# Order edits in a hybrid mLSTM / Mamba-2 layer: turns of one head, state copies, score weights, group sums, half-spreading products and the last row sums

## What is computed

```python
u = modulate(rmsnorm(x)); x = x + 0.5 * g1 * swiglu(u)          # ff1, 1024 x 2816
u = modulate(rmsnorm(x))
q, k, v, mo, i, f, z, xbc, dt, ga, gb = split(u @ w_in)
q, k = silu(conv4(q, k));  h = mlstm(q, k, v, i, f, state)       # 4 heads, 256 x 512 memory
h = (h - mean) * rsqrt(var + eps) * head_g * sigmoid(mo);  ya = h @ w_pa
x_, B, C = silu(conv4(xbc)); y = ssd(x_, dt, A, B, C, state) + D * x_   # 4 groups of 8 heads
y = y * silu(z); y = y * rsqrt(mean(y*y per group of 512) + eps) * norm_g; yb = y @ w_pb
x = x + g2 * ((sigmoid(ga) * ya + sigmoid(gb) * yb) @ w_out)
u = modulate(rmsnorm(x)); x = x + 0.5 * g3 * swiglu(u)           # ff2
y_out = rmsnorm(x, final_norm)                                   # plus the new states
```

## Time and profile before

| | |
|---|---|
| median of 3 runs | 1263.19 us (1263.02 to 1265.1) |
| the profiled execution's own time | 1262.8 us |
| its span in the profile | 1261.1 us |
| TensorE matmul busy | 1240.4 us, 98% of the span |
| VectorE, ScalarE, POOL busy | 62%, 49%, 18% |
| granted TensorE clock, mean | 0.993 of full speed |

### The profile page before, as it was taken

The page is one execution under the profiler, slowest core; times in us unless marked ns, Lnnn a source line. Parts: engine busy times, 40 slices in busy tenths (PEclk is TensorE's granted clock), DMA queues, the critical chain, the costliest instruction groups (busy, mean ns, idle before and its releaser), DMA issues. The chain is left out here.

```text
span 1261.1 us, 22606 instructions
## 1 busy us (share of the span) xinstructions
PE 1240.4 (98%) x9059; PEld 1144.7 (91%) x9059; DVE 783.3 (62%) x1345; ACT 620.8 (49%) x1102; POOL 220.8 (18%) x385
## 2 busy tenths in 40 slices
PE   8999999999999999999999999999999999999997
PEld 5999989998988777779999989989999999999997
DVE  4744444547976667675388787875676885455432
ACT  5523324335668555655356776565543453333432
POOL 5100000012640212130033333414200300000000
PEclk8999999999999999999999999999999999999998
DMA  9998879553324788986474558365454454653541
GB/s 310 264 345 261 260 252 300 158 167 127 117 85 145 254 299 306 355 272 173 140 206 129 158 153 243 105 206 155 127 138 152 152 190 145 200 160 111 161 138 42
DMA packets 258629, 241.54 MB, mean 192 GB/s; under 512 B 8205, under 2 KB 242141, under 8 KB 258526
## 3 DMA queue, kind: packets, MB, share of 16 engines
q1 hardware_dynamic: 249850, 211.16, 54.6%
q0 software_dynamic: 8576, 28.91, 6.8%
q10 hardware_dynamic: 100, 0.04, 0.0%
HBM read 209.88 MB, written 30.21 MB: 190 GB/s over the span
## 5 line engine op out<-in xcount | busy, mean ns | idle before, releaser
L2552 DVE TENSOR_TENSOR w_lo<-ring,w_hi 128x1024 fp32r<-128x1024 f32 (+1 forms) x264 | 337.6, 1279 | 354.4 <-ACT w_hi L1889 353.8
L1889 ACT ACTIVATE w_hi<-ring 128x1024 fp32r<-128x1024 f32 (+1 forms) x264 | 289.6, 1097 | 485.7 <-PE bank L1010 441.7
L1010 PE MATMUL bank<-u_hi,w_hi 128*128 128x320 f32 x1472 | 257.5, 316 | 0.7 <-ACT w_hi L1889 0.5
L1010 PE MATMUL bank<-u_hi,w_lo 128*128 128x320 f32 x1472 | 247.0, 310 | 0.4 <-DVE w_lo L2552 0.4
L1010 PE MATMUL bank<-u_lo,w_hi 128*128 128x320 f32 x1472 | 246.4, 310 | 0.0
L1010 PEld LDWEIGHTS bank<-u_hi,w_hi 128*128 128x128 f32 x1472 | 222.8, 188 | 16.3 <-issue 9.6
L1010 PEld LDWEIGHTS bank<-u_hi,w_lo 128*128 128x128 f32 x1472 | 223.7, 188 | 1.3 <-DVE w_lo L2552 1.2
L1010 PEld LDWEIGHTS bank<-u_lo,w_hi 128*128 128x128 f32 x1472 | 224.3, 188 | 0.1
L818 POOL TENSOR_TENSOR arena<-x_t,gain 128x64 f32<-128x64 f32 x16 | 4.8, 298 | 337.4 <-DVE x_t L2634 337.4
L1010 PE MATMUL bank<-ff_hi,w_hi 128*128 128x320 f32 x352 | 57.5, 310 | 0.0
L1010 PE MATMUL bank<-ff_hi,w_lo 128*128 128x320 f32 x352 | 56.8, 308 | 0.0
(11 more groups left out here) (426 smaller groups left out, 1682.1 us busy)
## 6 DMA issues: line engine op xcount, KB each, us to landing
ring<-in_w_in SPq DMA_DIRECT2D x52, 1024.0 KB, 5.4
ring<-in_ff_w SPq DMA_DIRECT2D x44, 1024.0 KB, 7.5
ring<-in_ff_w SPq DMA_DIRECT2D x32, 704.0 KB, 4.7
arena<-in_ada_w SPq DMA_DIRECT2D x20, 1024.0 KB, 10.0
ring<-in_ada_w SPq DMA_DIRECT2D x16, 1024.0 KB, 11.9
arena<-in_state_mlstm_C SPq DMA_DIRECT2D x22, 512.0 KB, 6.6
out_s_C<-arena POOLq DMA_DIRECT2D x22, 512.0 KB, 6.9
ring<-in_w_pa SPq DMA_DIRECT2D x8, 1024.0 KB, 8.0
```

Of the source, the lines that this page charges most:

```text
L1010: return nc.tensor.matmul(dst, lhs, rhs, start=first, stop=last)
L1889: nc.scalar.activation(w_hi[v.split_no % 2][:, 0:v.kc, :], panel_part(v), ACT.Copy).then_inc(S["hi_done"], 1)
L2552: V.tensor_tensor(w_lo[r][:, 0:v.kc, :], panel_part(v), w_hi[r][:, 0:v.kc, :].bitcast(FP32), ALU.subtract)\
```

## The change

It moves work, adds no instruction and takes none away. `i` is the place of a unit in its stage.

1. Stage 3 of the heads: head 2's tiles 8 to 11 are turned, gated and split at `i` = 4, 5, 6, 7, where it was 3, 4, 5, 6.
2. TensorE, groups: `head_outputs` stands ahead of `pack_inputs` (i = 2) and of `grown_decays` (i = 3).
3. VectorE, groups, i = 1: `sample_masks` stands behind `weights` and `outputs`.
4. ScalarE, i = 4, units other than `xbc` (only stage 3): `old_states(gr, 0)` stands ahead of the gate copy.
5. Tail: `group_sums(2)` moves from behind unit 3 into unit 4, behind its first eight products. `roots(0, 3)` on ScalarE and `group_roots(0, 3)` on VectorE move from unit 3's list to unit 4's. TensorE's `group_roots` stay behind unit 4.
6. End: the three products of the partly summed squares run before the wait for the last square, the other three after it; tile 1 comes last.

```diff
-TURN_SLOTS = ({}, {3: 0, 4: 1, 5: 2}, {0: 3, 3: 4, 4: 5, 5: 6}, {0: 7, 3: 8, 4: 9, 5: 10, 6: 11})
+TURN_SLOTS = ({}, {3: 0, 4: 1, 5: 2}, {0: 3, 3: 4, 4: 5, 5: 6}, {0: 7, 4: 8, 5: 9, 6: 10, 7: 11})
...
                     if i == 1 and gr > 0:
                         turn_old_part(gr - 1)
+                    if 1 <= i <= 4:
+                        head_outputs(gr, i - 1)
                     if i == 2:
                         pack_inputs(gr)
                     if i == 3:
                         grown_decays(gr)
-                    if 1 <= i <= 4:
-                        head_outputs(gr, i - 1)
...
             for i, u in enumerate(tail_units()):
-                dense(u)
+                dense(u, inner=(lambda: group_sums(2)) if i == 4 else None)
...
                 if i == 3:
                     group_sums(1)
-                    group_sums(2)
...
-            pe.wait_ge(S["sq_ready"], 4 * KD)
-            for c in range(3):
-                rows = 128 if c < 2 else 64
-                t = slice(c * 128, c * 128 + rows)
-                mm(aux[3][0:rows, c:c + 1], sq[:, 0, t], ones[:, 0:1], True, False)
-                ins = mm(aux[3][0:rows, c:c + 1], sq[:, KD - 1, t], ones[:, 0:1], False, True)
+            for kc in (0, KD - 1):
+                if kc > 0:
+                    pe.wait_ge(S["sq_ready"], 4 * KD)
+                for c in (0, 2, 1):
+                    rows = 128 if c < 2 else 64
+                    t = slice(c * 128, c * 128 + rows)
+                    ins = mm(aux[3][0:rows, c:c + 1], sq[:, kc, t], ones[:, 0:1], kc == 0 and c == 0, kc > 0 and c == 1)
...
                     high_ahead(u)
+                    if i == 4 and u.name != "xbc":
+                        old_states(gr, 0)
...
-                    if i == 4:
+                    if i == 4 and u.name == "xbc":
                         old_states(gr, 0)
...
-                if i == 3:
+                if i == 4:
                     roots(0, 3)
-                if i == 4:
                     squares(3)
...
-                    if i == 1:
-                        if gr > 0:
-                            old_part(gr - 1)
-                        sample_masks(gr)
+                    if i == 1 and gr > 0:
+                        old_part(gr - 1)
                     if i < 4 and not amid:
                         weights(gr, i)
                     if 1 <= i <= 3 and not amid:
                         outputs(gr, i - 1)
+                    if i == 1:
+                        sample_masks(gr)
...
-                if i == 3:
+                if i == 4:
                     group_roots(0, 3)
```

## The result

The changed kernel takes 1271.4 us (median of 4 runs, 1270.81 to 1272.56); the kernel before, on the same chip, 1263.51 us (4 runs, 1263.02 to 1265.1). The ratio is 1.0061, 95% interval 1.0044 to 1.0079: slower by 0.61%, 7.7 us (the medians differ by 7.9). The profiled execution of after took 1270.81 us with a span of 1268.8 us, 7.7 above the span before.

A forecast was written before the change was run, and what follows sets the result against it. TensorE, its matmul row busy 98% of the span, was taken as the bound, so time changes only where it stands still or runs slowly. Terms summed to +5.1 on the profiled 1262.8: 1267.9 us, range 1264.0 to 1270.2.

The forecast's parts named there:

- turns of head 2: Heads: new waits of 1.55 before the second `pa` unit and 1.8 before head 3's turns, 0.85 gained; net +2.55 us.
- clock behind it: Head 3's turns: the clock falls to half after the new waiting; +1.65 us, bounds 0 and 3.3.
- head outputs, masks: Groups, i = 2: the wait goes on both sides, 0.3 to 0.5 in each of four groups; -1.6 us.
- state copies: Group 3: the copy ahead of the gate removes the 1.01 us wait of `turn_states(3, 1)`; -1.1 us.
- tail, what goes: Tail: the idle 0.73 before the third group of sums and unit 4's half clock go; -2.4 us.
- tail, the wait: Tail, behind unit 4: TensorE waits for roots and reciprocals that stand behind unit 4's rounding and gate; +5.0 us.
- tail, clock behind it: Tail: the clock falls again behind the 5 us wait; +1.65 us, bounds 0.5 and 3.3.
- end: End: half of the 12 row-sum instructions move into the idle 1.30 ahead of the last square; -0.65 us.
- the rival that it is kept: Head 3's turns: the waits come but the clock stays full, dense work between them; 1266.3 us, chance 0.28.
- The rival that the `pick_x` products wait: Groups: masks end later than 737.1, so the half-spreading products wait in their new place; 1269.5 us, chance 0.09.
- roots in time: Tail: roots are ready before unit 4 ends, TensorE goes straight on; 1261.3 us, chance 0.09.
- A drain beside the table load: Tail wait: each of two table switches costs a drain beside its load; +2.8, 1270.7 us, chance 0.04.

The follow-up runs named there:

- Experiment 2: The changed kernel with the roots and reciprocals of groups 0 to 2 ahead of the rounding in unit 4's lists of the tail: 1261.96 us, ratio 0.9985.
- experiment 3: Also "wait filled": the changed kernel with 32 dense products, results unread, between unit 4 and the root products of the tail: 1268.19 us, ratio 1.0035.
- experiment 4: Also "unit 5 first": the changed kernel, with TensorE running unit 5 behind the same tail wait and the root products after it: 1270.06 us, ratio 1.0048.
- A: The changed kernel with all the edits, against the kernel before: 1271.4 us, ratio 1.0061.
- experiment 5: Also "roots before gate": the changed kernel with the tail's roots between unit 4's rounding and its gate copy, reciprocals likewise: 1270.28 us, ratio 1.0049.
- experiment 6: The kernel before with only head 2's turns moved to units 4 to 7: 1265.97 us, ratio 1.0021.
- experiment 1: Also "turns back": the changed kernel with head 2's tiles 8 to 11 back behind units 3 to 6: 1268.43 us, ratio 1.0037.
- the last kernel: The changed kernel with head 2's old turns, roots ahead of the rounding, and `grown_decays` ahead of `head_outputs` again at i = 3: 1258.51 us, ratio 0.9959.
- experiment 8: The kernel before with VectorE's order alone changed, `sample_masks` behind `weights` and `outputs`: 1266.44 us, single run.
- B: The kernel before the change: 1263.51 us, median of 4 runs beside the changed kernel.
- experiment 7: The kernel before with TensorE's order alone changed, `head_outputs` ahead of `pack_inputs` and `grown_decays`: 1266.15 us, single run.

## Why the prediction was wrong by 3.5 us, and where it was right

The forecast was 1267.9, in the range 1264.0 to 1270.2; the median is 1271.4, outside by 1.2. Slower was given 0.81 and came. The terms make 2.6 of the miss of 3.5; the rest is 0.3 of the execution's own time outside the span and 0.6 between that execution and the median. Term by term, from the shifts of the same row between the two traces:

| term | forecast | measured |
|---|---|---|
| turns of head 2 | +2.55 | +2.6 |
| clock behind it | +1.65 | 0 |
| head outputs, masks | -1.6 | -0.6 |
| state copies | -1.1 | -1.05 |
| tail, what goes | -2.4 | -2.35 (0.8 wait, 1.5 clock) |
| tail, the wait | +5.0 | +5.1 |
| tail, clock behind it | +1.65 | +4.6 |
| end | -0.65 | -0.6 |
| sum | +5.1 | +7.7 |

- **The failed step is the clock behind the tail's wait**: "the clock falls again ... so I take the seen loss, +1.65, bounds 0.5 and 3.3". The fall was right, its size was not: 4.6 lies beyond even the far bound of 3.3. I took the loss of one unit from the place where the clock fell before, though there a dense unit followed at once. Here 18 identity products follow. The clock fell at 896.9 and was back at 907.2; the work in between took 11.09 up to 908.11 in place of 6.52: 4.57 lost. Experiment 2 takes wait and clock away, 3 the clock alone; in 4, in the one execution traced, it is shorter with a dense unit first. That the wait and the clock behind it are this loss is shown; that the identity products are why the clock stays low so long rests on that one trace.
- **Clock at head 3's turns**: the rival that it is kept had 0.28 and was right; PEclk is 1.00 at both waits in A and in experiments 2 to 6, six traces. The waits are 1.66 and 1.34 with a dense unit between them. Had I taken both clock terms right, the forecast would have been 5.1 - 1.65 + 2.95 = +6.4, 1269.2. So the two errors on the clock offset each other in part: with this rival alone right, the forecast was 1266.3, further off than 1267.9.
- **Turns**: the chain of seven steps hit to 0.2 us: second `pa` unit forecast at 572.5, measured 572.68; head 3's turns 577.8 and 577.79. That the moved turns make the two waits, experiments 1 and 6 show from both sides; that it is tile 11 among the four is read from the rows (the turn at 567.02, the copy at 567.61, the gating at 571.51, the gate copy at 572.15) and was not tried alone.
- **Head outputs**: at i = 2 the wait went on both sides, 0.38 per group within the forecast 0.3 to 0.5, in three of four groups and 0.33 in the first. "At i = 3 nothing waited, so the exchange is worth 0" was wrong: 0.20 per group is lost there, which the last kernel gets back. Nothing idles in the trace at that point. In group 1 the decay rows are followed after 0.50 (743.73 to 744.23) where it was 0.41 (741.55 to 741.96), and the two `pick_b` products after 0.37 (745.15 to 745.51) where it was 0.27 (741.96 to 742.23); all other steps agree to 0.01. These two make the 0.20; why the order matters to them stays open. The rival that the `pick_x` products wait was wrong with both edits in, and is what VectorE's half alone does (experiment 8: 0.57 idle ahead of them).
- **State copies, tail what goes, end**: as forecast, to 0.05, from shifts of rows; none was tried alone. In "tail, what goes" that is partly luck. The prediction took it as given that the old wait of 0.73 costs the clock. The tail with that wait is in four traces: in B's and experiment 8's trace unit 4 then runs at half clock, in those of experiments 6 and 7 it does not (rows under "Short waits"). Against such an execution the term is worth 0.8, and only against one like B's trace 2.35.
- **The wait of the tail**: forecast T + 5.0, measured T + 5.10, with T = 891.92. The rival "roots in time" (0.09) was wrong as to this kernel; its condition, that the roots do not stand behind the rounding, is the right one: with the roots ahead of the rounding (experiment 2) the wait is gone.
- **A drain beside the table load** was wrong. The gate copy starts at 894.55 behind a load from 893.25 of 1.28, and the root at 896.30 behind one from 895.00: 0.02 left over. No drain shows, neither behind the loads nor ahead of the second, which starts 0.01 behind the end of the gate copy. The Trainium skill ("ScalarE: Activation LUTs", What ACT_TABLE_LOAD costs) puts 1.38 of drain beside the load. By an estimate from that figure, two drains would have made this wait 7.9; it is 5.1.

## What to carry to other kernels

Before an instruction is moved one place down in a list, ask whether what now stands ahead of it is a prefetch that waits for the end of the very work it should run beside; on an in-order engine a few instructions of 0.2 us then cost the full chain, here 5.1 us. Price the clock behind a wait apart from the wait, and by what runs first afterwards: here the wait of 5.1 us in front of identity products cost 4.6 more, dense work in the wait, even useless, took that away, and a dense unit directly behind it took some 2.8 of it away in the one execution traced. A half clock seen once in a trace is one execution's: see whether it comes back in others before a change is credited with removing it. Where two engines' orders are changed together, neither half can be judged alone: here each lost about 0.46 per group and both together gained 0.38.

## What the runs showed of the hardware

**How long the clock stays low.** From windows of half a microsecond, one traced execution of each kernel, with the loss taken against the 6.52 us that root products and unit 5 take at full clock (893.23 to 899.75 in experiment 2):

| kernel | idle | clock at half | runs first | half until, behind the first dense product | lost |
|---|---|---|---|---|---|
| A | 4.94 | 896.9 to 907.2 | identity | 4.8 | 4.57 |
| turns back | 4.94 | 894.1 to 904.3 | identity | 3.3 | 3.88 |
| roots before gate | 3.20 | 897.0 to 907.2 | identity | 4.1 | 4.26 |
| unit 5 first | 4.94 | 894.7 to 901.5 | dense | 4.0 | 1.79 |
| wait filled | 0.26 | never | - | - | 0.1 |

In all four the clock came back 3.3 to 4.8 us after the first dense unit began; in three of them it had stood at half through 5.3 us of identity products before that. The loss is 0.45 of the time worked at half clock in each of them (10.2, 8.6, 9.4 and 4.0 us). Where in the wait the clock falls varies too: 0.1 ahead of its end in the first row, 1.6 in the second, 0.8 in the third and 2.9 in the fourth, so the stretches of the third column also hold waiting. Why the clock did not rise during the identity products is open; it was not tried.

**Short waits.** 1.66 and 1.34 with a dense unit between them cost no clock in six traces. 0.73 between one-column products was followed by half clock in two traces (B and experiment 8) and not in two others (experiments 6 and 7). Timeline and window of TensorE in experiment 6, around the wait and unit 4:

```profile
889.58 0.81 PE L1010 MATMUL aux<-ones,arena 128*128 128x1 f32 x6 [0.73 <-POOL arena L986]
890.32 1.44 PE L1010 MATMUL bank<-u_hi,w_hi 128*128 128x320 f32 x8
```

```profile
889.00:893.00 4.00, 3.42 (x24) 1.00 0.21 62
```

So the wait is not enough by itself, and what else decides is open. In the eight traces that have a tail without that wait, no half clock stands at unit 4 before the new wait.

**The start of the kernel.** Identical code before the first edit does not take the same time. The products with `vp` start at 540.27 in the profile before, 540.30 in A and 540.25 in the last kernel, and in all twelve traces between 539.81 and 542.84. The granted clock over the first 30 us differs as well (0.89, 0.94 and 1.00 in the three named), but does not order them: the trace of experiment 3 has 1.00 and 542.43. What makes the difference of 3 us is open. It is why the terms above are read as shifts between rows and the kernels compared by medians.
